# Sliding-window attention inside a one-layer trunk: softmax and transposes over 128 columns, values as the stationary operand

## The reference

```
h    = rmsnorm(x) * (1 + scale) + shift            # adaLN from the conditioning vector
qkv  = h @ w_qkv + b                               # 16 query heads, 4 key/value heads, head size 64
per block of 128 queries and its 256 keys (128 of the block before, 128 of its own):
  scores = q . k + rel_bias, kept where 0 <= distance < 128
  probs  = softmax([scores, sink])[without the sink]
  out    = probs @ v
x    = x + gate * (out @ w_o + b_o)
x    = x + gate2 * moe(rmsnorm(x) ...)             # top 4 of 32 experts, clamped SwiGLU
out  = rmsnorm(x)
```

## Time and profile before

| what | value |
|---|---|
| median of three runs | 1999.17 us |
| profiled execution, its own time | 1994.97 us |
| its span, first to last instruction | 1993.4 us |
| TensorE busy, share of the span | 98% |
| VectorE / ScalarE / GpSimd busy | 32% / 23% / 11% |
| attention pipeline | about 170 to 490 us |
| experts | about 500 us to the end |
| mean granted TensorE clock | 0.993 |

### The profile page before, as it was taken

How to read it: one execution, slowest core, us unless ns; L and a number is a source line. 1 busy time by engine, 2 the same in 40 slices (tenths; PEclk the granted TensorE clock), 3 DMA queues, 4 the chain that set the end, 5 groups by cost and what they waited for, 6 DMA issues and landing times.

```text
span 1993.4 us, 52573 instructions
## 1 busy us (share of the span) xinstructions
PE 1951.8 (98%) x23835; PEld 1765.1 (89%) x23835; DVE 643.2 (32%) x1860; ACT 455.4 (23%) x1286; POOL 217.3 (11%) x250
## 2 busy tenths in 40 slices
PE   7999999999999999999999999999999999999997
PEld 4756875554999999999999999999999999999997
DVE  2645545565242222222213222222222222222224
ACT  3103433441121212121111111111212111112213
POOL 2003000000011010101111011111110101100002
PEclk9999999998999999999999999999999999999998
DMA  9880111102988798878888888889797998999986
GB/s 362 308 176 7 43 44 75 43 33 104 355 295 322 273 343 286 322 275 310 289 318 290 311 303 311 323 289 339 262 369 251 364 328 319 339 327 340 324 320 222
DMA packets 150213, 524.05 MB, mean 263 GB/s; under 512 B 10026, under 2 KB 15810, under 8 KB 149986
## 3 DMA queue, kind: packets, MB, share of 16 engines
q1 hardware_dynamic: 131186, 467.68, 64.9%
q0 software_dynamic: 17200, 52.59, 7.7%
q10 hardware_dynamic: 1600, 0.36, 0.1%
HBM read 485.34 MB, written 34.21 MB: 261 GB/s over the span
## 4 chain that ended last, share of the span: by engine, by line
PE 93%; DMA 2%; DVE 2%; SPq 1%; issue 1%; ACT 1%; POOL 0%; ACTq 0%; DVEq 0%; POOLq 0%
PE ps L1656 46%; PE ps L1690 23%; PE ps L1505 5%; PE ps L1442 4%; PE ps L1512 3%; PE ps L1644 2%; PE ps L1630 2%; PE ps L1480 1%; PE ps L1420 1%; PE ps L1465 1%; PE ps L1438 1%; DMA ring<-in_w_qkv 1%; DMA ring<-in_moe_w 1%; ACT ring L706 0%; SPq L407 0%
## 5 line engine op out<-in xcount | busy, mean ns | idle before, releaser
L1656 PE MATMUL ps<-U,ring 128*64 128x120 f32 (+11 forms) x13312 | 935.9, 270 | 2.5 <-DMA ring<-in_moe_w 1.9
L1656 PEld LDWEIGHTS ps<-U,ring 128*64 128x64 f32 (+1 forms) x13312 | 923.0, 149 | 10.8 <-issue 8.5
L1690 PE MATMUL ps<-U,ring 128*64 128x120 f32 (+11 forms) x6656 | 469.2, 270 | 1.7 <-issue 1.6
L1690 PEld LDWEIGHTS ps<-U,ring 128*64 128x64 f32 (+1 forms) x6656 | 461.8, 149 | 6.1 <-issue 5.3
L1229 DVE TENSOR_SCALAR U<-ps,U 128x120 f32<-128x120 f32 (+11 forms) x256 | 90.7, 354 | 1092.6 <-PE ps L1656 1092.6
L808 ACT ACTIVATE U<-U 128x120 f32<-128x120 f32 (+11 forms) x256 | 80.2, 313 | 889.9 <-DVE U L1229 889.9
L819 ACT ACTIVATE U<-ps,U,modT 128x120 f32<-128x120 f32 (+11 forms) x256 | 119.0, 465 | 289.1 <-PE ps L1690 288.9
L570 POOL DMA_INDIRECT acc_d<-U x43 | 43.2, 1005 | 766.3 <-DVE U L1221 762.6
L1505 PE MATMUL ps<-ring 128*128 128x512 f32 x256 | 116.2, 607 | 0.0
L1505 PEld LDWEIGHTS ps<-ring 128*128 128x128 f32 x256 | 48.1, 193 | 59.3 <-issue 59.2
L794 ACT ACTIVATE U<-ps,modT,Af 128x120 f32<-128x120 f32 (+11 forms) x252 | 91.9, 469 | 9.2 <-PE ps L1630 9.2
(11 more groups left out here) (229 smaller groups left out, 1137.9 us busy)
## 6 DMA issues: line engine op xcount, KB each, us to landing
ring<-in_moe_w SPq DMA_DIRECT2D x191, 2048.0 KB, 10.0
U<-in_w_mod SPq DMA_DIRECT2D x8, 2048.0 KB, 11.7
ring<-in_w_mod SPq DMA_DIRECT2D x3, 2048.0 KB, 19.4
ring<-in_w_qkv SPq DMA_DIRECT2D x3, 2048.0 KB, 18.8
acc_d<-xr SPq DMA_DIRECT2D x10, 512.0 KB, 2.8
xr<-in_x SPq DMA_DIRECT2D x8, 512.0 KB, 9.2
ring<-in_w_o SPq DMA_DIRECT2D x2, 2048.0 KB, 7.8
xn_d<-U SPq DMA_DIRECT2D x8, 512.0 KB, 2.6
```

The source lines that it names most:

```text
L1656: last = pe.matmul(bank(j % 4)[lo:hi, s * 256:s * 256 + n], w[:, k, s, (j % 2) * P + lo:(j % 2) * P + hi], xT[:, k, 0:n], start=(k == 0), ...
L1690: last = pe.matmul(bank(m % 4)[lo:hi, 0:n], w[:, k, (m % 4) * P + lo:(m % 4) * P + hi], actT[:, k, 0:n], start=(k == 0), stop=(k == KT - 1))
```

## The change

- The add of the bias is as before. In blocks 1 to 7 VectorE then takes the larger of the two keys' scores at each place, into the second 128 columns; row maximum, exponentials and transposes run over these 128 columns alone.
- The probabilities are normalised before the transpose: `denominators(u)` on VectorE in step u, then `normalise(u)` on ScalarE, four scaled copies of 128x128. TensorE's `probs_transpose(u)` waits for them.
- VectorE alone takes the transposed probabilities out of PSUM, once times a mask for the own block and, in blocks 1 to 7, once times its complement for the block before. The two masks are made once.
- The product has the values stationary, the same 64 columns in both column tiles, and streams 256 columns of probabilities into each; its result is already transposed. `heads_out` and `heads_transpose` go away.
- q products and projections alternate between banks 7 and 5. `o_gate` on VectorE comes after `scores_in`, not before.

```diff
             def exps(u):
-                z = 0 if u // NKV else P
                 act.wait_ge(s_nm, u + 1)
                 for r in range(GRP):
-                    act.activation(scores[:, u % 2, r, z:], scores[:, u % 2, r, z:], ACT.Exp,
+                    act.activation(scores[:, u % 2, r, P:], scores[:, u % 2, r, P:], ACT.Exp,
...
-            def probs_evacuate(u):
...
+            def normalise(u):
+                act.wait_ge(s_rec, u + 1)
+                for r in range(GRP):
+                    last = act.activation(scores[:, u % 2, r, P:], scores[:, u % 2, r, P:], ACT.Copy,
+                                          scale=rec[:, u % 2, r:r + 1])
+                last.then_inc(s_nrm, 1)
+
+            def attn_evacuate(u):
                 b, g = u // NKV, u % NKV
-                act.wait_ge(s_ot, u + 1)
+                act.wait_ge(s_pv, u + 1)
...
             for u in range(STEPS):
-                if 1 <= u <= UNITS:
-                    probs_evacuate(u - 1)
+                if u < UNITS:
+                    normalise(u)
                 if 2 <= u <= UNITS + 1:
-                    heads_evacuate(u - 2)
+                    attn_evacuate(u - 2)
...
-                link(dve.tensor_reduce(out=mx[:, u % 2, :], in_=s, axis=AX.X, op=ALU.max))
+                wrapped = scores[:, u % 2, :, P:]
+                if b:
+                    link(dve.tensor_tensor(out=wrapped, in0=wrapped, in1=scores[:, u % 2, :, 0:P], op=ALU.max))
+                link(dve.tensor_reduce(out=mx[:, u % 2, :], in_=wrapped, axis=AX.X, op=ALU.max))
...
-                src = bank(5).rearrange("p (h k n) -> p h k n", h=2, k=2)
-                dst = probsT[:, u % 2, 512:1024].rearrange("p (h k n) -> p h k n", h=2, k=2)
-                dve.tensor_copy(dst[:, :, lo_k:, :], src[:, :, lo_k:, :]).then_inc(s_ptv, 1)
+                src = bank(4).rearrange("p (h n) -> p h n", h=GRP)
+                for v in range(2 if u // NKV else 1):
+                    last = dve.tensor_tensor(out=probsT[:, u % 2, v, :].rearrange("p (h n) -> p h n", h=GRP), in0=src,
+                                             in1=key_mask[:, v:v + 1, :].to_broadcast([P, GRP, P]), op=ALU.mult)
+                last.then_inc(s_ptv, 1)
+
+            def denominators(u):
+                dve.wait_ge(s_exp, u + 1)
...
             for u in range(STEPS):
                 if 1 <= u <= UNITS:
                     probs_out(u - 1)
-                if u - 1 in o_half:
-                    o_gate(*o_half[u - 1])
+                if u < UNITS:
+                    denominators(u)
                 if u + 1 < UNITS:
                     scores_in(u + 1)
                 if u - 1 in o_half:
+                    o_gate(*o_half[u - 1])
                     residual(*o_half[u - 1])
...
-                if 1 <= u <= UNITS:
-                    heads_out(u - 1)
...
             def probs_transpose(u):
-                pe.wait_ge(s_exp, u + 1)
+                pe.wait_ge(s_nrm, u + 1)
...
-                    for kb in range(0 if u // NKV else 1, 2):
-                        last = pe.transpose(bank(4, 2)[:, (place * 2 + kb) * P:(place * 2 + kb + 1) * P],
-                                            scores[:, u % 2, place, kb * P:(kb + 1) * P], ident[:, :])
+                    last = pe.transpose(bank(4)[:, place * P:(place + 1) * P], scores[:, u % 2, place, P:], ident[:, :])
...
-                for place in range(GRP):
-                    first = 0 if b else 1
-                    for kb in range(first, 2):
-                        at = (place * 2 + kb) * P
-                        for lo, hi in QUERY_HALVES:
-                            last = pe.matmul(bank(6)[lo:hi, place * HD:(place + 1) * HD], probsT[:, u % 2, at + lo:at + hi],
-                                             vv[:, b - 1 + kb, g * HD:(g + 1) * HD], start=(kb == first), stop=(kb == 1))
+                parts = [(0, b), (1, b - 1)] if b else [(0, b)]
+                for v, t in parts:
+                    for a in range(2):
+                        last = pe.matmul(bank(6)[64 * a:64 * a + 64, 0:256], vv[:, t, g * HD:(g + 1) * HD],
+                                         probsT[:, u % 2, v, 256 * a:256 * a + 256], start=(v == 0), stop=(v == len(parts) - 1))
...
             def q_product(m, z):
-                pe.wait_ge(s_qa, len(by_act) + 2 * m + z)
+                if m or z:
+                    pe.wait_ge(s_qa, len(by_act) + 2 * m + z - 1)
...
-                if 1 <= u <= UNITS:
-                    heads_transpose(u - 1)
```

More of the change, by code:

```diff
@@ L108, in program @@
         scores = ring[:, late:late + 2048].rearrange("p (b h n) -> p b h n", b=2, h=GRP)
-        heads = ring[:, late + 2048:late + 2560].rearrange("p (b n) -> p b n", b=2)
+        key_mask = ring[:, late + 2048:late + 2304].rearrange("p (v n) -> p v n", v=2)
         gated = ring[:, late + 2560:late + 3072]
@@ L114, in program @@
         macc = ring[:, late + 3840:late + 4096].rearrange("p (t e) -> p t e", t=TT)
-        probsT = ring[:, 5 * PIECE:5 * PIECE + 2048].rearrange("p (b n) -> p b n", b=2)
+        probsT = ring[:, 5 * PIECE:5 * PIECE + 2048].rearrange("p (b v n) -> p b v n", b=2, v=2)
         gmB = ring[:, 5 * PIECE + 2048:5 * PIECE + 3072]
@@ L349, in o_bank, with q_bank @@
         def o_bank(t, h):
-            return bank(1) if (t, h) == (LAST, 1) else bank(7)
+            return bank(1) if (t, h) == (LAST, 1) else bank(7 - 2 * h)
+        def q_bank(n):
+            return bank(7 - 2 * (n % 2))
         def head_at(place):
@@ L775, in _ @@
                     act.wait_ge(s_qkv, len(groups) + u)
-                    act.activation(qT[:, 1, m, z * 256:z * 256 + 256], bank(7)[:, 0:256], ACT.Identity, scale=0.125,
+                    act.activation(qT[:, 1, m, z * 256:z * 256 + 256], q_bank(u - 1)[:, 0:256], ACT.Identity, scale=0.125,
                                    bias=bq8[:, m:m + 1])\
@@ L963, in _ @@
                 dve.tensor_scalar(diag[:, n, :], ident[:, :], col, None, ALU.mult).then_inc(s_dg, 1)
+            link(dve.tensor_tensor(out=key_mask[:, 0, :], in0=tri[:, :], in1=ident[:, :], op=ALU.add))
+            dve.tensor_scalar(key_mask[:, 1, :], key_mask[:, 0, :], -1.0, 1.0, ALU.mult, ALU.add).then_inc(s_km, 1)
+            dve.wait_ge(s_km, 1)
             dve.wait_ge(s_bc, 2 * KT)
@@ L986, in probs_out @@
             def probs_out(u):
-                lo_k = 0 if u // NKV else 1
                 dve.wait_ge(s_ptr, u + 1)
@@ L1470, in pv_product @@
                 b, g = u // NKV, u % NKV
-                pe.wait_ge(s_pta, u + 1)
                 pe.wait_ge(s_ptv, u + 1)
@@ L1474, in pv_product @@
                     pe.wait_ge(s_at, u)
-                for place in range(GRP):
-                    first = 0 if b else 1
-                    for kb in range(first, 2):
-                        at = (place * 2 + kb) * P
-                        for lo, hi in QUERY_HALVES:
-                            last = pe.matmul(bank(6)[lo:hi, place * HD:(place + 1) * HD], probsT[:, u % 2, at + lo:at + hi],
-                                             vv[:, b - 1 + kb, g * HD:(g + 1) * HD], start=(kb == first), stop=(kb == 1))
-                last.then_inc(s_pv, 1)
-            def heads_transpose(u):
-                pe.wait_ge(s_o, u + 1)
-                for z in range(2):
-                    last = pe.transpose(bank(6)[:, z * P:(z + 1) * P], heads[:, u % 2, z * P:(z + 1) * P], ident[:, :])
-                last.then_inc(s_ot, 1)
+                parts = [(0, b), (1, b - 1)] if b else [(0, b)]
[3 more added lines that the diff above has]
+                                         probsT[:, u % 2, v, 256 * a:256 * a + 256], start=(v == 0), stop=(v == len(parts) - 1))
+                last.then_inc(s_pv, 1)
             pe.wait_ge(s_qa, len(by_act))
@@ L1499, in o_product @@
                     pe.wait_ge(s_sadd, UNITS)
-                elif t or h:
-                    pe.wait_ge(s_gt, 2 * t + h)
+                elif t:
+                    pe.wait_ge(s_gt, 2 * t if t == LAST else 2 * t + h - 1)
                 else:
@@ L1509, in q_product @@
             def q_product(m, z):
-                pe.wait_ge(s_qa, len(by_act) + 2 * m + z)
+                if m or z:
+                    pe.wait_ge(s_qa, len(by_act) + 2 * m + z - 1)
                 for k in range(KT):
-                    last = pe.matmul(bank(7)[:, 0:256], wq[:, k, m * P:(m + 1) * P], hT[:, k, 512 + z * 256:768 + z * 256],
+                    last = pe.matmul(q_bank(2 * m + z)[:, 0:256], wq[:, k, m * P:(m + 1) * P], hT[:, k, 512 + z * 256:768 + z * 256],
                                      start=(k == 0), stop=(k == KT - 1))
```

24 lines of the change are left out of this document (3 added, 21 removed).

## The result

The changed kernel took 1979.08 us (median of four runs, 1975.98 to 1980.95), the kernel before beside it 1997.56 us (1992.33 to 1999.92). The ratio is 0.9914, 95% interval 0.9898 to 0.993: about 17 us faster, where 11 were forecast.

A forecast was written before the change was run, and what follows sets the result against it. TensorE's own work sets the pace to about step 27, then a chain over VectorE and ScalarE. 14.5 us at full clock less 3.5 for the clock gives 11 less: 1984 us profiled, 1988 median; range 1981 to 1998.

The forecast's parts named there:

- the own time: Whole kernel: sums made against the profiled 1994.97 us; the median of runs lies 4.2 us above, added at the end.
- the clock: Falls of TensorE's clock expected at the start of most of steps 25, 27, 29, 31; 3.5 us net lost, between -2 and 11.5.
- the sum at full clock: All pipeline stretches from step 0 to the projection after step 32, without clock falls: 14.5 us gained.
- Steps 0 to 23: TensorE's own work sets the pace; its step falls by 0.66 us, to 6.24 in steps 5 to 15; 13.6 us gained.
- Rivals 3 and 4: 3: column tiles do not overlap, 2007 us, chance 0.07; 4: steps 5 to 15 not shortened, 1995 us, chance 0.05.
- The factor of 2 of the Trainium skill: Value product: by the skill's column tiling it would fall to 0.54 us, some 15 us more; the prediction rejected this.
- Steps 0 to 4: First transposes wait for normalise(0), 1.4 us lost; with regained transposes and idle time, net gain 1.0 us (-0.5 to 2).
- Steps 24 to 32: Transposes wait for normalise: steps 24 to 27 lose 3.6 us, 28 gains 3.0, 29 and 30 lose 1.8, 31 and 32 gain 3.3.
- The fall at 450.9: Today's second clock fall, around short waits among transposes and narrow products; counted as already in the time.
- The rival with the clock holding: Rival 1: clock holds and late waits are shorter (normalise 1.2 us); gain 16 to 18, 1982 us, chance 0.2.

The follow-up runs named there:

- fillers: Changed kernel with two useless full-width matmuls on TensorE behind the logits of steps 24, 26, 28 and 30; 1999.99 us, 0.993 to the kernel before.

## Why the prediction was right in its steps and wrong in its time

The mechanism was right, and three terms were mis-sized, all to the same side. The measured median is 9 us under the forecast of 1988: 6.1 us from the own time that was added, 3.4 from the clock, 3.4 from the sum at full clock; against them stand 3.1 us of the first stage and 0.7 before the experts. The range went wrong by the own time.

- **Steps 0 to 23**: right in kind. 6.17 us for the 6.24 forecast; the transposes and heads' transposes as forecast, the value product 0.06 us shorter where I took nothing. Steps 5 to 23 gained 13.7 us, where 12.6 were forecast. Extra work on TensorE counts in full, extra work on VectorE not at all. Rivals 3 and 4 fall.
- **The factor of 2 of the Trainium skill** (TensorEngine Tiling (Array Packing), "When to Use Tiling"): 1.02 for 1.08 us by starts. The old product already used both column tiles, its halves of 64 queries, and its 64-column passes overlapped, as the rows before let one read; the factor did not come.
- **Steps 0 to 4**: the first wait grew by 1.6 us for 1.4 forecast. I did not think of a clock fall behind it. In both traces of the changed kernel it came and cost 1.6 us; in those with fillers and with the gate moved, which have the same code up to step 5 and the same wait, it did not.
- **Steps 24 to 32**: right in place and releaser (1.70 us of wait on normalise for 2.0), which is shown by moving the copies. The rows of the table agree to 0.4 us, but in part by luck, since the measured ones hold falls. At full clock steps 24 to 27 lose 2.6 us (even steps 14.1 for the 14.4 forecast, odd 11.2 for 11.4), not 3.6, and step 28 takes 9.7 us (9.74 with one bank, where no fall is near), not 9.45: with the fall of step 27 it began 0.8 us later and its wait ended no later.
- **The step that failed in the profiled execution is the clock**, "Taken: 3.5 us net". I let most odd steps fall. Two did. That of step 27 cost nothing, as the trace with fillers shows: step 28 waits for ScalarE, and this slack I did not see. That of step 29 cost 0.6 us (its transposes took 413.34 - 412.29 = 1.05 us for 0.58, the step 11.34 for 11.20). The fall at 450.9, which I counted as in the time, did not come: 2.1 us back in step 33. With the 1.6 at step 0 the clock took 0 + 0.6 + 1.6 - 2.1 = 0.1 us, not 3.5. Another execution gives another figure: by the trace with the third masked copy, with late falls of 3.3 us and none at step 0, it is 1.2. Why no fall came in step 31 of the changed kernel is open: waits of 1.70, 0.71, 0.47 and 0.57 us stand there, and with one bank or the third copy it did fall there. The rival with the clock holding had the better size for a partly wrong reason: the clock fell, and it hardly mattered.
- **The sum at full clock** was 14.5 us; with the falls taken out of the table's rows it is 17.9. No term was far off, but nearly each erred to the same side: 1.0 us in steps 0 to 4, 1.1 in 5 to 23, 1.0 in 24 to 27, -0.3 in 28, 0.6 after it. With the clock this gives 11 + 3.4 + 3.4 - 0.7 - 3.1 = 14.0 us, the difference of the two profiled executions.
- **The own time failed too**, "The median of the runs shown is 4.2 us above it; I add that at the end". The changed kernel's median lies 1.9 us under its profiled time, so this step missed by 6.1 us, more than any other. 3.1 us of this is the fall in its first stage, if the other runs do not have it, which no trace shows; the rest is within what runs of the kernel before scatter (8 us). The distance of one execution from the median is a property of that execution and not of the kernel. The range had no term for this, and so ended 2 us too high.

## What to carry to other kernels

Where one engine paces a stretch, price an edit by the starts of that engine, and find the place where the pace passes to a ring over the others: there the same edit has the other sign, and one instruction's place in another engine's order (masked copies ahead of add_list, the gate behind the add) decides several us. Charge a clock fall only with what is left of it behind the next wait that another engine ends, be it a step later. Before carrying a sum from one profiled execution to the median, look how far that execution is from the median, and put that distance into the range.

## What the runs showed of the hardware

- The place of a clock fall varies between executions of the same instructions: of traces with the same code up to step 5 and the same wait of 2.33 us, the changed kernel's two show a fall (29.48 us to step 5), and those with fillers from step 24 and with the gate moved show none (27.84). In the first stage a fall came at a DMA wait of 0.52 us in three executions and cost 3 us; four others waited 0.51 to 0.53 us there without a fall at it.
- What a fall costs depends on the next wait: 1.6 us at step 0, where TensorE's work is the path; 0.6 in step 29; nothing in step 27, since TensorE waits for ScalarE in step 28 (29.97 us from step 26 to the end of that wait, with the fall and without).
- On the three chips of the experiments the experts take 1507 to 1511 us instead of 1489.5, with the same instructions and a granted clock of 1.00. From 1200 to 1400 us TensorE is busy 200.00 us of the changed kernel's first trace and 198.9 of its second; short pauses without a releaser lie between. The cause is open.
- Useless matmuls that keep an engine busy are doubled by a low clock like any other, 3.78 us for 1.98.
